# Ten further rooms for experts' weights instead of six, some filled from the stage ahead on, and a modulation half worked off in the routing

## The reference

```python
def hier_moe(h, router_g, router_g_b, router_e, router_e_b, w_gate, w_up, w_down):
    # top-1 of 4 groups, then top-2 of its 8 SwiGLU experts (width 256)
    g_logits = xt @ router_g + router_g_b
    g_prob = softmax(g_logits); _, g_top = top_k(g_logits, 1)
    p_group = take_along_axis(g_prob, g_top)
    e_logits = einsum('td,gde->tge', xt, router_e) + router_e_b
    e_sel = take_along_axis(e_logits, g_top)
    top_v, top_i = top_k(e_sel, 2)
    top_w = softmax(top_v) * p_group
    ...
    for gi in range(4):
        hid = silu(einsum('td,edf->tef', xt, w_gate[gi])) * einsum('td,edf->tef', xt, w_up[gi])
        out = out + einsum('tef,efd->td', hid * gates[:, gi], w_down[gi])
```

## Time and profile before

| | |
|---|---|
| median of three runs | 3541.01 us (3537.59 to 3548.04) |
| profiled execution | 3533.29 us, span from first to last instruction 3531.5 us |
| TensorE busy | 3108.5 us, 88% |
| mean granted clock of TensorE | 0.946 |
| first `Moe`: routing, then expert passes | 590 to 618.6 us, 618.6 to 911.3 us |
| second `Moe`: routing, then expert passes | 1259 to 1288 us, 1288 to 1574.4 us |
| near expert loads (SP) | 192 of 1 MB, drawn ones (POOL) 90 |

### The profile page before, as it was taken

One profiled execution on the slowest core, in us unless ns is written; L12 is line 12 of the kernel. 1 busy time (PEld: TensorE's weight loads), 2 busy tenths in 40 slices (PEclk: granted clock), 3 DMA queues, 4 the chain that ended last, 5 costly groups with the idle time before them and its releaser, 6 DMA issues. The chain is left out here.

```text
span 3531.5 us, 54798 instructions
## 1 busy us (share of the span) xinstructions
PE 3108.5 (88%) x24140; PEld 2389.0 (68%) x24140; DVE 1412.3 (40%) x2665; ACT 1083.5 (31%) x1725; POOL 310.6 (9%) x460
## 2 busy tenths in 40 slices
PE   7888886878899778878999898999999998898998
PEld 5776765323698653336777676777677876777998
DVE  5455565111344631124333334333343333435554
ACT  4344443111343321123222223222232223225443
POOL 0122220111000011110000110000100000000000
PEclk9899997989899989999999999999999999999999
DMA  6323334878666068873444323444332222213452
GB/s 254 132 92 134 118 113 167 331 288 343 245 227 217 11 257 341 330 280 131 149 167 155 133 88 127 149 167 155 113 107 90 96 90 90 96 36 108 155 186 102
DMA packets 113629, 580.06 MB, mean 164 GB/s; under 512 B 24048, under 2 KB 26608, under 8 KB 60400
## 3 DMA queue, kind: packets, MB, share of 16 engines
q1 hardware_dynamic: 66160, 449.96, 34.2%
q0 software_dynamic: 47232, 126.60, 10.0%
HBM read 669.79 MB, written 1.05 MB: 190 GB/s over the span
## 5 line engine op out<-in xcount | busy, mean ns | idle before, releaser
L352 PE MATMUL ps<-t,t 128*128 128x512 f32 (+1 forms) x3488 | 1223.0, 351 | 114.3 <-DVE t L546 53.2
L353 PE MATMUL ps<-t,t 128*128 128x512 f32 (+1 forms) x3488 | 1211.5, 347 | 0.0
L354 PE MATMUL ps<-t,t 128*128 128x512 f32 (+1 forms) x3488 | 1210.1, 347 | 0.0
L329 DVE TENSOR_TENSOR t<-t,t 128x1024 fp32r<-128x1024 f32 x448 | 549.4, 1230 | 780.9 <-ACT t L310 780.7
L352 PEld LDWEIGHTS ps<-t,t 128*128 128x128 f32 x3488 | 668.4, 192 | 223.9 <-issue 70.4
L354 PEld LDWEIGHTS ps<-t,t 128*128 128x128 f32 x3488 | 668.6, 192 | 85.6
L353 PEld LDWEIGHTS ps<-t,t 128*128 128x128 f32 x3488 | 669.2, 192 | 81.7
L310 ACT ACTIVATE t<-t 128x1024 fp32r<-128x1024 f32 x448 | 469.6, 1054 | 589.9 <-PE ps L354 581.1
L1336 PE MATMUL ps<-t,t 128*32 128x512 f32 x1504 | 216.1, 626 | 33.9 <-DMA t<-in_experts_dram 26.7
L684 POOL DMA_DIRECT2D t<-in_wmod_dram x224 | 118.7, 536 | 1247.2 <-PE ps L633 1130.7
L1358 PE MATMUL ps<-t,t 128*32 128x512 f32 x752 | 147.2, 701 | 52.5 <-DMA t<-in_experts_dram 43.3
(11 more groups left out here) (309 smaller groups left out, 2959.3 us busy)
## 6 DMA issues: line engine op xcount, KB each, us to landing
t<-in_wall_dram SPq DMA_DIRECT2D x221, 1024.0 KB, 4.9
t<-in_experts_dram SPq DMA_DIRECT2D x192, 1024.0 KB, 8.8
t<-in_wmod_dram POOLq DMA_DIRECT2D x224, 512.0 KB, 5.8
t<-in_wmod_dram SPq DMA_DIRECT2D x16, 512.0 KB, 12.9
t<-in_wall_dram SPq DMA_DIRECT2D x10, 512.0 KB, 3.9
t<-in_lora_dram POOLq DMA_DIRECT2D x8, 512.0 KB, 3.9
t<-in_rcst_dram POOLq DMA_DIRECT2D x1, 1536.0 KB, 6.5
t<-in_experts_dram,t POOLq DMA_INDIRECT x90, 4.8
```

What stands on the lines that cost most here:

```text
L329: e.tensor_tensor(lo, self.raw(n), hi, ALU.subtract).then_inc(*net.wlo.up((self.name, n)))
L352: e.matmul(out, lh, rh, start=start, stop=False, **kw)
L353: e.matmul(out, lh, rl, start=False, stop=False, **kw)
L354: return e.matmul(out, ll, rh, start=False, stop=stop, **kw)
```

## The change

It does five things. (1) MORE goes from 6 to 10: eight rooms in the arena and two lent from `mring`, whose four places of 1024 floats make two rooms. The lent ones wait for the mark "mods room" and carry near slots only. Short-lived routing tensors share the second gather buffer's memory (`brief`), and `Bc`, `A`, `B`, `fars` move into fixed tensors that are free then. (2) Four of the arena rooms serve the drawn slots; after the first 13 near slots ten rooms remain for the near ones. (3) Arena rooms that lie above the memory of the stage before (`ended`) are gated by the start of that stage: two in layer 0, eight in layer 1. They come first in the order, and the router's slot is put behind them. (4) One modulation half is worked off in the routing of each `Moe`, and GpSimd loads the next half's chunks when the lent rooms are done with. (5) The second gather of a pass uses bank 1 instead of 3.

```diff
-MORE = 6
+MORE = 10
...
-        self.s_drawn = [sem(f"s_drawn{i}") for i in range(4)]
+        self.s_drawn = [sem(f"s_drawn{i}") for i in range(8)]
...
-    def more_rooms(self, aps, stage):
-
-        for j, ap in enumerate(aps):
-            self.rooms[NS + j], self.turn[NS + j], self.gates[NS + j] = ap, len(self.slots) - 1 + (j + 1) / (MORE + 1), stage
+    def more_room(self, x, ap, turn, stage=None, key=None):
+
+        room = NS + x
+        self.rooms[room], self.turn[room] = ap, turn
+        if stage is not None:
+            self.gates[room] = stage
+        if key is not None:
+            self.freed[room] = (self.sums, key)
...
-    def fewer_rooms(self, first=0, n=0):
-
-        self.rooms = {x: ap for x, ap in self.rooms.items() if x < NS or NS + first <= x < NS + first + n}
+    def fewer_rooms(self, which):
+        for x in which:
+            del self.rooms[NS + x]
...
+        ended = net.top
         net.top = net.arena
-        more = [f(SW) for _ in range(MORE)]
...
+        self.Ug = [v3(f(2048), 256)]
+        at = net.top + -net.top % 8
+        self.Ug.append(v3(f(2048), 256))
+        brief = net.take(1248, at=at)
...
+        self.Bc = net.ULf[:, 3072:4096]
+        self.A, self.B = net.sqsum[:, 0:256], net.sqsum[:, 256:512]
+        self.fars = v3(net.rstd[:, 0:256], 128)
...
-        net.more_rooms(more, i)
+        more = []
+        for x in range(8):
+            net.top += -net.top % 8
+            early = net.top >= ended
+            more.append(f(SW))
+            net.more_room(x, more[x], x - 100 if early else len(net.slots) - 1 + x / 16, stage=i - 1 if early else i)
+        for x in range(8, MORE):
+            net.more_room(x, net.mring[:, SW * (x - 8):SW * (x - 7)], len(net.slots) + x, key=("moe", layer, "mods room"))
+        first = [x for x in range(8) if net.turn[NS + x] < 0]
+        drawn = (first + [x for x in range(8) if x not in first])[0:4]
+        self.router = None
...
+                if near == len(first) and self.router is None:
+                    self.router = net.slot(*router)
+                if near == NS + MORE - 1:
+                    net.fewer_rooms(drawn)
                 if x >= 32:
-                    self.w[n, t, s] = net.drawn_slot(t, more[t], ("block", x - 32, s), net.sums, key)
+                    self.w[n, t, s] = net.drawn_slot(drawn[t], more[drawn[t]], ("block", x - 32, s), net.sums, key)
                 else:
-                    if near == NS + MORE:
-                        net.fewer_rooms(4, MORE - 4)
...
-        net.fewer_rooms()
+        net.fewer_rooms([x for x in range(MORE) if x not in drawn])
+        self.mods_rooms = [net.freed[NS + x] for x in range(8, MORE)]
...
@@ pe_route
+        net.bg_pe.go(e, w, 1, at=6)
+        net.sums.note(("moe", self.l, "mods room"))
         b = self.take(w, 0, "places")
...
+        net.bg_pe.go(e, w, 1, at=7)
@@ pe
             if g < 6:
-                self.pe_gather(e, w, g, kk + 1, 3)
+                self.pe_gather(e, w, g, kk + 1, 1)
@@ act
         net.acts.note(("moe", self.l, "tokens high"))
+        net.bg_act.go(e, w, 2)
@@ dve
         self.dve_gates(e, w)
+        net.bg_dve.go(e, w, 2)
         self.dve_choice(e, w, 1)
@@ pool
         self.pool_blocks(e, w)
+        for marks, key in self.mods_rooms:
+            w.wait_ge(*marks.of(key))
+        net.bg_pool.go(e, w, 2)
```

More of the change, by code:

```diff
@@ L731, in __init__ @@
         self.turn, self.filled, self.freed, self.gates = [x - NS for x in range(NS)] + [0] * MORE, [0] * (NS + MORE), {}, {}
-        self.drawn = [0] * 4
+        self.drawn = [0] * 8
         self.cst = self.take(NC_)
@@ L1239, in __init__ @@
         self.es, self.oh1, self.oh2, self.inn = (v3(f(16), 8) for _ in range(4))
[L1240 to L1243, removed]
         self.pos = v3(f(64), 32)
[L1245 to L1248, removed]
+        self.bid, self.ids = f(15), net.take(45, mybir.dt.uint32)
         self.V8 = f(8)
         self.w1, self.w2 = self.V8[:, 4:6], self.V8[:, 6:8]
-        self.Bc = f(1024)
-        self.A, self.B = f(256), f(256)
         self.gs = f(2)
-        self.fars = v3(f(256), 128)
         self.S = [net.rview(256) for _ in range(2)]
-        self.Ug = [v3(f(2048), 256) for _ in range(2)]
         self.sg, self.h, self.hT = f(256), f(256), f(256)
+        self.cst = f(MSMALL.shape[1])
+        self.Ug = [v3(f(2048), 256)]
+        at = net.top + -net.top % 8
+        self.Ug.append(v3(f(2048), 256))
+        brief = net.take(1248, at=at)
+        part = lambda n, o: brief[:, o:o + n]
+        self.tmp = part(64, 0)
+        self.both, self.picked = part(128, 64), part(128, 192)
+        self.M, self.upM = v3(part(64, 320), 32), v3(part(96, 384), 32)
+        self.D, self.far = v3(part(64, 480), 32), v3(part(64, 544), 32)
+        self.over, self.upto, self.shift = part(32, 608), part(32, 640), part(32, 672)
+        self.cmp = part(480, 704)
+        self.rowf = v3(part(45, 1184), 3)
+        self.Bc = net.ULf[:, 3072:4096]
+        self.A, self.B = net.sqsum[:, 0:256], net.sqsum[:, 256:512]
+        self.fars = v3(net.rstd[:, 0:256], 128)
         hi, lo = (t.rearrange("p c t -> p (c t)") for t in (net.UH, net.UL))
@@ L1261, in __init__ @@
         self.G = [v3(lo[:, 2048 + 512 * x:2560 + 512 * x], 256) for x in range(2)]
-        self.cst = f(MSMALL.shape[1])
-        self.router = net.slot(([("moe_router_g", (layer,), 128 * k, 0, 4, 36 * k) for k in range(8)]
+        router = (([("moe_router_g", (layer,), 128 * k, 0, 4, 36 * k) for k in range(8)]
                                 + [("moe_router_e", (layer, g), 128 * k, 0, 8, 36 * k + 4 + 8 * g) for k in range(8) for g in range(4)]),
-                               288, net.sums, ("moe", layer, "router"))
-        net.more_rooms(more, i)
+                  288, net.sums, ("moe", layer, "router"))
+        more = []
[9 more added lines that the diff above has]
+        self.router = None
         self.w = {}
@@ L1742, in pool_blocks @@
                     e.indirect_dma_start(ap, None, rows, bass.IndirectOffsetOnAxis(ap=self.ids[:, 3 * x + s:3 * x + s + 1], axis=0),
[L1743 removed]
+                                         bounds_check=12288 * self.l + 12287, oob_is_err=False).then_inc(net.s_drawn[room - NS], 16)
 class RwkvCore(Stage):
```

## The result

The changed kernel takes 3490.17 us (median of four, 3487.04 to 3511.73) where the kernel before takes 3539.99 us: a ratio of 0.9868, 95% interval 0.9826 to 0.9911, 50 us less. The profiled execution takes 3489.51 us instead of 3533.29, so 43.8 us less. Forecast were 3475 us, 66 us less, in a range of 3424 to 3514.

The account below looks back on a forecast made before the run. Too few near rooms let the DMA engines run dry in the expert stages; 226 + 25 + 8 = 259 us a stage, so 33.7 + 27.4 + 5 (modulations) = 66 us off, 3475 us, range 3424 to 3514.

Parts of the forecast that it names:

- What bounds the kernel: Expert stretches: with six near rooms the DMA engines run dry between bursts, the 15 to 18% their share lacks.
- The floor of 226 us: Expert stretch with ten near rooms: lasts at least 226 us, of which 84 loads at 2.48 us are 208.3.
- Late landings in bursts, 8 us: Near bursts: some fourth loads land 1.2 us late, at most 14 us a stage, of which 8 were taken.
- Far passes, 25 us: Four far passes a stage: near queue idles 0 to 12.5 us each behind drawn loads; middle 6.2 taken, 25 in all.
- How long four drawn loads take beside a near stream: Far passes: about 4 us to the first packet plus 12.8 us at 45 packets a us, 16.8 us.
- The second and third step both stall: Far passes: second and third step start drawn loads late, so 9.7 and 11.0 us show; a pass of 37 us.
- Filled from the stage ahead on, 0: Arena rooms filled before the expert stage: 0 beyond the eleventh load, as nothing waited for weights before the first expert matmul.
- A modulation half in the routing, 5 us: Routing gaps hold one half a layer; two halves fewer in a feed-forward stage win 5 us.
- The second gather's bank: Ten passes a layer: the turn no longer waits 0.69 us for ScalarE's copy; slack, 0, at best 14 us.
- The DMA limit: Rival, chance 0.17: drawn loads not slowed beyond what near rooms hide; 226 us a stage, 132 us off, 3409 us.
- A lower rate of a long stream: Rival, chance 0.03: a load takes 2.9 us when the stream doesn't pause; stage 294 us, 3545, no measurable change.
- Starving far blocks: Rival, chance 0.06: drawn loads served only once the near queue is empty; 306 us a stage, 3569 us, slower.

Follow-up runs that it names:

- 4: Changed kernel with six further rooms instead of ten, none lent from the modulations, all else of the change kept: 3556.09 us, 1.0058 of the kernel before.
- 3: Kernel before the change without its 45 drawn loads a layer and the waits for them: 3514.64 us, 0.9941 of the kernel before.
- 2: Changed kernel without its 45 drawn loads a layer and the waits for them: 3413.88 us, 0.9642 of the kernel before.
- 1: Changed kernel with one pool of fourteen rooms shared by near and drawn slots, drawn ones issued several steps ahead: 3411.53 us, 0.9651 of the kernel before.
- 12: Changed kernel with the shared pool of fourteen rooms and without filling from the stage ahead on: 3405.19 us, 0.9608 of the kernel before.
- 8: Changed kernel with all arena rooms gated by the Moe stage itself, none filled from the stage ahead on: 3516.09 us, 0.9948 of the kernel before.
- 9: Changed kernel without early filling, near loads behind a far pass waiting until the far blocks' down weights have landed: 3481.77 us, 0.9817 of the kernel before.
- 7: Changed kernel with the second gather of a pass in bank 3 again: 3499.03 us, 0.9888 of the kernel before.

## Why the prediction was right, and where it was off

The direction, the place and the range were right; of the forecast 66 us, 44 came in the profiled execution, and 50 by the medians. Of the signs named for being right, near waits shrank to a third and drawn ones grew, though to 5.6 us a far pass of idle time and not 8; but the DMA share stayed under 0.9 (0.86 and 0.88) and the stretches 11.3 and 5.9 us above 259. Step by step:

- *What bounds the kernel.* Right. Near rooms were the bound: waits for near weights fell by two thirds, with six rooms the gain is gone (4), and in 3 and 2, where no drawn load disturbs, going from six to ten near rooms gives 54.8 and 47.6 us a stretch.
- *The floor of 226 us.* Right. Three kernels that hardly or never wait for drawn loads show 227.6 and 231.5 (2), 230.9 and 231.4 (1), 228.0 and 228.6 us (12).
- *Late landings in bursts, 8 us.* Too much: what 2 has above 226 us is 1.6 and 5.5 us, and holds everything else too.
- *Far passes, 25 us.* **The step that failed in size.** The drawn loads cost 42.7 and 33.4 us (2), 10.7 and 8.4 us a far pass. I had bounded the near queue's idle time at 12.5 us a pass and taken the middle, 6.2. By the queue's busy share its idle time is 47.3 us in the first stretch and 8.4 in that of 2, and 37.8 against 8.2 in the second: 9.7 and 7.4 us a far pass. That this lies within my bounds is in part luck, as both terms of the upper one were too large: a far pass of 37 us (17 + 20.7 is 37.7) took 27.1 to 34.3, and the near rooms, which I took to be filling for 24.8 us, kept the queue busy for some 18 us behind the scatter (664.4 to 682.7), since part of them held landed weights when the stall began (an estimate: 18.3 us at 2.53 us a load are seven loads, not ten). The half-speed clock of the stall, 0.50 above, was no term at all. The reason I gave for the middle, that an idle queue serves drawn loads fast again, is true of the down step (2.1 to 2.4 us from issue to landing for three of the four in 8), but it comes too late: by then all near rooms are given out, and the queue stays idle till TensorE frees one. This term, 17.7 and 8.4 us too low against 6.4 and 2.5 too much for late landings, turns 259 into 270.3 and 264.9.
- *How long four drawn loads take beside a near stream.* I said 16.8 us, by 144 packets at 45 a us. Measured are 15.6 us from the first issue at 660.6 to the fourth at 676.2, in other pieces: 8.0 us to the first, then 2.53 to 2.56 us each. My 3.2 us a load was wrong: four drawn loads are served at one near load each, which takes 2.53 us in a long stream. A near load is 144 of the profile's packets too (12446 for 90.69 MB above), 9 for each of the 16 engines, as a drawn one is. The Trainium skill ("DMA: Bandwidth & Descriptors", Queues, rings and completion order) says that an engine finishes a packet of typically some 9 to 17 descriptors of one queue before it turns to the next. The trace agrees, 2.53 to 2.56 us apart; the 13.9 us that I worked out by it is low since the first load waits 8.0 us.
- *The second and third step both stall.* Half right. In five of the changed kernel's six full far passes only the second step stalls for long, and they take 27.1 to 29.2 us from one scatter to the next (the first 28.0, 664.36 to 692.36); in the other both stall, 34.3 us. In 8 both stall in all six, 32.0 to 37.9 us (the first 33.7, 648.85 to 682.51). Which it is, 1 to 2 us in the order of issue decide (8 and 9). I had not seen that the forecast hung on this.
- *Filled from the stage ahead on, 0.* Right as to the filling (12 is as fast without it as 1), wrong as to the edit: in this kernel it moved the order of issue, and so carried 25 us (8), and with six rooms it comes with a pause of SyncE (4). The cost of an edit that renumbers slots isn't that of its purpose.
- *A modulation half in the routing, 5 us.* The fit into the routing was right; the gain is seen only in part. The first rows of its step stand in the gap ahead of the places, which still wait 2.0 us (3.9 before), and the feed-forward stage has two halves fewer, 96 and 12 records in the same part of the stage as the earlier trace rows:

```profile
603.69 1.93 PE L633 MATMUL ps<-t,t 128*32 128x256 f32 x32
607.64 0.43 PE L1425 MATMUL ps<-t,t 128*128 128x96 f32 x2 [2.02 <-DVE t L1586]
...
608.11 0.61 PE L640 MATMUL ps<-t,t 128*128 128x128 f32 x4
```

```profile
L633 PE MATMUL ps<-t,t 128*32 128x256 f32 x96 | 5.8, 382 | 0.0
L640 PE MATMUL ps<-t,t 128*128 128x128 f32 x12 | 1.8, 272 | 0.0
```

  The records are 3.9 and 0.6 us fewer, 4.5 us, and routing has not grown. But what lies behind the second stretch took 1957.1 us before and 1954.9 us now, 2.2 us less, and with 1.2 us more between the layers and 1.3 ahead of them none of it is left in the profiled execution as a whole. Over all runs this last part takes 1957.1 and 1957.6 us in the two kernels without the moved halves (before and 3) and 1953.2 to 1956.3 us in those with them: 1 to 4 us.
- *The second gather's bank.* 0, at best 14: inside (7 shows 0 to some 9 us), nearer is not known.
- *The rivals.* The DMA limit, 3409 us, is reached in the kernels of 1 and 2, 3411.5 and 3413.9 us, where drawn loads don't hold TensorE; the changed kernel doesn't get there. A lower rate of a long stream is out: in 1 the near queue is 95.7% busy over 230.9 us for 91.44 MB, 2.53 us for a load of 1.05 MB, against 2.48 in a short burst. Starving far blocks exist in a mild form: one near load for each drawn one, not the whole queue.

What stays open: why in the changed kernel SyncE's burst starts 1.4 us after the step that frees its rooms has ended (687.3 against 682.24 + 3.64), and in 8 at once (671.3 against 667.59 + 3.64). The released slots are of the same steps in both. SyncE is not the one that is late: by the trace's semaphore events TensorE's signal came at 687.30, 1.4 us after the step's modelled end, and SyncE issued at once; in 8 the signal came at 671.28. That the order decides is shown by 9; what delays the signal is not.

## What to carry to other kernels

- A small transfer in a second queue isn't small beside a stream that never pauses: here each waited for one load of the stream. Issue it a stream's depth ahead, from the same rotation of buffers, or let the stream yield for it. Deepening only the stream makes it dearer: here from some 9 to some 38 us a stage.
- Where the cost of an unseen collision has a lower and an upper bound, ask what happens in the time in which the collision is over: if the other side's buffers are full by then, as here, a fast service afterwards gives nothing back.
- Before an edit is costed at 0 because of what it is for, list what else it reorders. An ablation that loses time is not yet the worth of the part that was taken out: look which pass got slower.

## What the runs showed of the hardware

- A drawn load with all its rows out of bounds, 144 packets with next to no bytes, lands 2.1 us after issue with an idle near queue, 5.5 us when a near load is issued 0.4 us after it (8). Behind a full near queue TensorE gets four of them 2.53 to 2.56 us apart (changed kernel).
- The near queue kept 2.53 us a load over 230 us on end (1; 405 GB/s in the window), 2% above a burst of seven.
- While TensorE waited for drawn loads its granted clock went from 1.00 (668 to 670 us) to 0.50 (672 to 674 us), 2.4 to 1.2 GHz, and the far step's last 26 records took 4.57 us (6.58 in 8), where a whole unstalled step of 32 takes 3.64.
